# First block's rows fetched ahead and picked on TensorE, and the last expert block's results by token

## What is computed

```python
x = x + mix @ w_out                     # mix = [mLSTM(h) | pool(h)], h = rmsnorm(x, norm1_g) @ w_in
x = x + hier_moe(rmsnorm(x, norm2_g))   # top-1 group, top-2 experts in it
y = rmsnorm(x, norm_f_g)

def hier_moe(x, ...):
    gates = ...                          # (B, L, 16), two entries of a token are not zero
    for e in range(16):
        hid = silu(x @ w_gate[e]) * (x @ w_up[e])      # width 512
        y = y + gates[..., e:e + 1] * (hid @ w_down[e])
```

## Time and profile before

| what | us |
|---|---|
| median of 3 runs | 955.98 |
| the profiled execution | 955.15 |
| its span, first to last instruction | 953.5 |
| TensorE busy | 881.4 (92%) |
| DVE busy | 435.6 (46%) |
| GpSimd busy | 370.2 (39%) |
| ScalarE busy | 145.7 (15%) |
| mean granted TensorE clock | 0.966 of full |

### The profile page before, as it was taken

One profiled execution on the slowest core, in us unless ns is written; L12 is line 12 of the kernel. 1 busy time (PEld: TensorE's weight loads), 2 busy tenths in 40 slices (PEclk: granted clock), 3 DMA queues, 4 the chain that ended last, 5 costly groups with the idle time before them and its releaser, 6 DMA issues. The chain is left out here.

```text
span 953.5 us, 16776 instructions
## 1 busy us (share of the span) xinstructions
PE 881.4 (92%) x6367; PEld 758.9 (80%) x6367; DVE 435.6 (46%) x1168; ACT 145.7 (15%) x447; POOL 370.2 (39%) x569
## 2 busy tenths in 40 slices
PE   5999999999999999999986799999999999999920
PEld 3975969779596795968853399999999999999920
DVE  2245474737537365463656723334333333333255
ACT  2123122221312212121121000000000000000051
POOL 4050040300303012030220466678887777764512
PEclk9999999999999999999989799999999999999975
DMA  9931101020300202011065169999999999999882
GB/s 334 287 128 20 49 14 32 1 78 2 70 8 12 67 1 56 1 13 44 1 192 173 50 212 312 343 348 359 336 350 343 332 334 329 321 310 301 244 326 114
DMA packets 90713, 163.27 MB, mean 171 GB/s; under 512 B 48834, under 2 KB 59570, under 8 KB 82463
## 3 DMA queue, kind: packets, MB, share of 16 engines
q1 hardware_dynamic: 72047, 138.25, 41.4%
q0 software_dynamic: 17568, 24.23, 11.1%
q10 hardware_dynamic: 1040, 0.00, 0.1%
HBM read 139.39 MB, written 25.44 MB: 173 GB/s over the span
## 5 line engine op out<-in xcount | busy, mean ns | idle before, releaser
L1428 PE MATMUL bank<-wout,win 128*128 128x130 f32 (+3 forms) x2048 | 246.4, 282 | 3.2 <-DVE wout L1316 3.2
L1428 PEld LDWEIGHTS bank<-wout,win 128*128 128x128 f32 x2048 | 244.8, 191 | 3.2 <-DVE wout L1316 3.2
L1428 PE MATMUL bank<-hT,win 128*128 128x128 f32 (+1 forms) x1536 | 182.9, 279 | 0.0
L1428 PEld LDWEIGHTS bank<-hT,win 128*128 128x128 f32 x1536 | 178.6, 192 | 1.5 <-issue 1.2
L582 POOL DMA_INDIRECT z_d<-wout,win x75 | 119.2, 1589 | 27.9 <-issue 26.6
L1428 PE MATMUL bank<-win 128*128 128x130 f32 (+3 forms) x1024 | 123.7, 281 | 0.0
L1428 PE MATMUL bank<-win,hT 128*128 128x260 f32 (+3 forms) x512 | 119.9, 412 | 3.2 <-DMA win<-in_w_in 1.7
L1428 PEld LDWEIGHTS bank<-win 128*128 128x128 f32 x1024 | 122.3, 190 | 0.0
L1428 PE MATMUL bank<-wout,mixT 128*128 128x512 f32 (+1 forms) x384 | 116.8, 487 | 1.8 <-ACT mixT L819 1.7
L1428 PEld LDWEIGHTS bank<-win,hT 128*128 128x128 f32 (+1 forms) x512 | 76.1, 171 | 41.8 <-issue 32.7
L1428 PEld LDWEIGHTS bank<-wout,mixT 128*128 128x128 f32 (+1 forms) x384 | 50.8, 163 | 57.1 <-issue 54.4
(11 more groups left out here) (296 smaller groups left out, 813.1 us busy)
## 6 DMA issues: line engine op xcount, KB each, us to landing
win<-in_w_gate SPq DMA_DIRECT2D x32, 1024.0 KB
win<-in_w_up SPq DMA_DIRECT2D x32, 1024.0 KB
win<-in_w_down SPq DMA_DIRECT2D x32, 1024.0 KB
win<-in_w_in SPq DMA_DIRECT2D x4, 2048.0 KB, 19.6
xbuf<-in_x_prompt SPq DMA_DIRECT2D x8, 512.0 KB, 3.9
wout<-in_w_out SPq DMA_DIRECT2D x1, 4096.0 KB, 15.5
z_d<-xbuf SPq DMA_DIRECT2D x32, 128.0 KB
h_d<-xn SPq DMA_DIRECT2D x8, 512.0 KB, 2.8
```

The lines of the kernel that those rows point to most:

```text
L1428: return nc.tensor.matmul(out, lhsT, rhs, start=first, stop=last)
```

## The change

Two things are done, with what they need.

**Block 1's rows.** GpSimd reads the ids of block 1 and gathers its rows after tile 6's scatter, into a buffer of its own (xg1). Rows that belong to tiles 7 and 8 are not in them: their slots still point to the zero row. DVE transposes (first_turn) and scales (first_scale) these during tile 8's mixing. For tiles 7 and 8 a selection matrix is made in places (first_picks on DVE: 1/rms where a token's place is this slot), and TensorE multiplies x1 (copied by ScalarE into xp) with it, which gives the missing columns already transposed; DVE adds both (first_rows), ahead of the table. The rows of h2_d for tiles 7 and 8 are filled with x beforehand by one DMA, and GpSimd's first wait counts that one too. The zero rows are written from one column of the empty table. The state copies go from DVE to ScalarE, and the stores of the states from SyncE's queue to ScalarE's; the state transposes stand in the wait for the routing of tile 8, and WARM is gone.

**The last block.** Its down projection has the tokens on the partitions: hid is the stationary operand, the weights are moved in 512 columns, for two tiles of 120 and 30 rows. DVE adds gate times result to the gathered rows of z_d straight from PSUM; last_d and its transfers are gone. The gathered rows are brought into plain order by eight copies first, and this wait (base_in) now stands ahead of the outputs.

```diff
-    last_d = nc.dram_tensor("last_d", [BLOCK, D], F32).ap()
...
+        PICKED = (LAST - 1, LAST)
...
+        PICKB = ((2, 0, 3), (3, 3, 6), (0, 6, 8))
...
-        FROWS = (P, BLOCK - P)
+
+        FROWS = ((NP - 1) * RP, RP)
+        FBANK = ((5, 6), (7, 1))
...
-        WARM = 14
...
-                sp.dma_start(rows[TOK, :].rearrange("(p n a) -> p n a", p=P, a=2), empty[:, 0:D // (2 * P), :]
-                             ).then_inc(S["ids_zeroed"], 16)
+                sp.dma_start(rows[TOK, :].rearrange("(p n a) -> p n a", p=P, a=1), empty[:, 0:D // P, 1:2],
+                             allow_slow_non_contiguous=True).then_inc(S["ids_zeroed"], 16)
             load_x(3)
+
+            early = [START[t] for t in PICKED]
+            sp.dma_start(h2_d[min(early):max(early) + P, :], x_prompt[0, min(early):max(early) + P, :]).then_inc(S["ids_zeroed"], 16)
...
+                if t == PICKED[0]:
+                    after(sp, "ids_zeroed", 16 * 4)
...
             after(pool, "hist_ready", 1)
-            after(pool, "ids_zeroed", 16 * 3)
+            after(pool, "ids_zeroed", 16 * 4)
...
+                if i == LAST:
+
+                    after(pool, "h2_stored", 16 * (LAST - 1))
+                    after(pool, "u_done", NT)
+                    load_ids(0)
+                    pool.wait_ge(ids_in, 16)
+                    add_quarter(False)
+                    pool.wait_ge(carried, 1)
+                    gather_tokens(first, xg1)
...
+                if t in PICKED:
+                    a.activation(xp[t - PICKED[0]], xbuf[:, t % 4, :].rearrange("p (f k) -> p k f", k=KD), ACT.Copy
+                                 ).then_inc(xp_ready, 1)
...
+            def first_picks(t):
+
+                i, place = t - PICKED[0], rt[:, 80:81]
+                link(v.scalar_tensor_tensor(out=rt[:, 128 + i:129 + i], in0=oh[:, t, 2, 0:1], scalar=-NEAR, in1=place,
+                                            op0=ALU.mult, op1=ALU.add))
+                v.tensor_scalar(pick[i], place_of[:, :, :], rt[:, 128 + i:129 + i], sm[:, 11:12], ALU.is_equal, ALU.mult
+                                ).then_inc(pick_ready, 1)
...
+            def first_rows():
+                dve.wait_ge(base_scaled, 1)
+                after(dve, "out_done", NT)
+                for n, (b, k0, k1) in enumerate(PICKB):
+                    dve.wait_ge(picked, n + 1)
+                    for k in range(k0, k1):
+                        at = B[b][:, (k - k0) * BLOCK:(k - k0 + 1) * BLOCK].rearrange("p (a i) -> p a i", a=NP)
+                        v.scalar_tensor_tensor(out=xgT[:, k, :, 0:RP], in0=at, scalar=g2m[:, k:k + 1], in1=xgS[:, k, :, 0:RP],
+                                               op0=ALU.mult, op1=ALU.add).then_inc(gx_ready, 1)
...
                     h2_evac(LAST - 1)
+                    first_turn()
                     numerators(LAST)
...
                     routing(LAST - 1)
+                    first_scale()
                     residual(LAST)
...
-            gather_turn(1)
             products(1, SLOTS[0][0])
+            gather_turn(1)
...
+            def add_last(i, c, n_done):
+
+                n, cols = FROWS[i], slice(c * (D // 2), (c + 1) * (D // 2))
+                dve.wait_ge(last_done, n_done)
+                return v.scalar_tensor_tensor(out=fy[i][0:n, cols], in0=B[FBANK[i][c]][0:n, :], scalar=fid[0:n, i, 1:2],
+                                              in1=fy[i][0:n, cols], op0=ALU.mult, op1=ALU.add)
...
             products(nblocks, RP)
+            dve.wait_ge(base_in, 16 * 2)
+            for i, n in enumerate(FROWS):
+                for q in range(NQ):
+                    link(v.tensor_copy(fy[i][0:n, :].rearrange("p (m q i) -> p m q i", m=KD, q=NQ)[:, :, q, :],
+                                       fb[i][0:n, q * PIECE:(q + 1) * PIECE].rearrange("p (m i) -> p m i", m=KD)))
             dve.wait_ge(nf_in, 16)
             outputs(0)
-            results(nblocks, RP, sooner + 2)
+            add_last(1, 0, 1)
+            add_last(1, 1, 1).then_inc(mixed, 1)
             outputs(1)
...
+            add_last(0, 0, 2)
+            add_last(0, 1, 3).then_inc(mixed, 1)
             outputs(2)
...
+                if i == NT + 1:
+                    first_picks(LAST - 1)
+                    state_transposes()
                 if 2 <= i:
                     ranks(i - 2)
+                if i == NT + 1:
+                    first_picks(LAST)
...
+            for half in range(2):
+                pe.wait_ge(hid_ready, 4 * nblocks + FH * (half + 1))
+                pe.wait_ge(w_loaded[4 + half], 16 * nblocks)
+                for c in range(2):
+                    last = by_token(1, c, range(half * FH, (half + 1) * FH))
+            last.then_inc(last_done, 1)
+            for c in range(2):
+                by_token(0, c, range(KF)).then_inc(last_done, 1)
```

More of the change, by code:

```diff
@@ L212, in hymba_step @@
         assert off + KD * NP * 32 <= 15 * D
+        PICKED = (LAST - 1, LAST)
+        xp = [win[:, (15 + i) * D:(16 + i) * D].rearrange("p (k f) -> p k f", k=KD) for i in range(2)]
+        xg1 = win[:, 17 * D:17 * D + NP * PIECE].rearrange("p (a d) -> p a d", a=NP)
+        pick = [win[:, 19 * D + i * BLOCK:19 * D + (i + 1) * BLOCK].rearrange("p (a i) -> p a i", a=NP) for i in range(2)]
+        PICKB = ((2, 0, 3), (3, 3, 6), (0, 6, 8))
         yb = [win[:, t * D:(t + 1) * D] for t in range(NT)]
@@ L406, in _ @@
             after(sp, "table_ready", 1)
[L407 to L417, removed]
-            sp.dma_start(pool_sample[0, 0], uout[:, 1, :]).then_inc(S["stores"], 16)
             nblocks = sp.value_load(tabi[0:1, 2 * (NB + 1):2 * (NB + 1) + 1], min_val=NE, max_val=NB)
@@ L661, in _ @@
             last = row_of(nblocks)
-            for i, n in enumerate(FROWS):
-                pool.dma_start(fid[0:n, i, :], ids_d[bass.ds(last + i * P, n), :]).then_inc(fid_in, 16)
+            pieces = ids_d[bass.ds(last, BLOCK), :].rearrange("(i a) n -> a i n", a=NP)
+            for a in range(NP):
+                i, at = (0, a * RP) if a < NP - 1 else (1, 0)
+                pool.dma_start(fid[at:at + RP, i, :], pieces[a]).then_inc(fid_in, 16)
             pool.wait_ge(carried, 7 * sooner + 13)
             add_block(sooner + 2, RP, 7 * sooner + 13)
-            pool.wait_ge(fid_in, 16 * 2)
+            pool.wait_ge(fid_in, 16 * NP)
             f = [0]
@@ L1046, in places @@
                 v.tensor_tensor(cnt[:, :], B[7][:, NE:2 * NE], cnt[:, :], ALU.add).then_inc(S["rank_read"], 1)
+                if t in PICKED:
+                    first_picks(t)
                 for n in range(2):
@@ L1177, in _ @@
             link(v.tensor_scalar(ecap[:, :], iof[:, 0:NE], float(CAP), None, ALU.mult))
+            for a in range(NP):
+                v.tensor_scalar(place_of[:, a, :], iof[:, 0:RP], float(NP), a - NEAR, ALU.mult, ALU.add)
             p0 = 0
@@ L1248, in _ @@
                     norm_x1(i - 1)
-            after(dve, "ulT_done", 1)
-            for n in range(2):
-                last = v.tensor_copy(uout[:, n, :], B[4 + n][0:HIST, :])
-            last.then_inc(S["ul_out"], 1)
-            after(dve, "nT_done", 1)
-            v.tensor_copy(gt[:, :, :], B[6][0:H, 0:2 * P].rearrange("p (a b) -> p a b", a=2)).then_inc(S["nT_out"], 1)
+            first_rows()
             NJ = NB + 1
@@ L1337, in _ @@
                 dve.sem_inc(signal, credit)
-            first_turn()
             def products(j, r):
```

159 lines of the change are left out of this document (96 added, 63 removed).

## The result

The changed kernel took 979.98 us (median of 4 runs, 978.26 to 983.31) beside 955.48 us for the kernel before on the same chip: ratio 1.0266, 95% interval 1.0246 to 1.0285. Forecast were 951.2 us and a range of 944.5 to 958. The profiled execution took 983.31 us with a span of 981.3 us, 27.8 us more than the span before; what follows accounts for these 27.8 us. TensorE is busy for 884.4 us (881.4 before): the time went into waits and into matmuls at half clock, not into work.

The account below looks back on a forecast made before the run. TensorE hardly waits from 100 to 480 us, so the start, the mixer-to-experts step and the end, where DVE matters, decide. Step 7.1 plus end 3.3 minus start 5.6 gains 4.8 us: 951.2 us, range 944.5 to 958.

Parts of the forecast that it names:

- The start: Before GpSimd's first copy: 256-row copy and 4-byte zero pieces delay GpSimd and TensorE, cost 5.6 us, bounds 2 to 9.4.
- rival D: At the start, the HBM-to-HBM copy moves at 165 GB/s: 955.0 us, no change to measure; chance 0.14.
- B: At the start, the copy is hidden by overlap or dlt has more room: 5.6 us more gained, 945.6; chance 0.12.
- Half clock behind the long idle stretch: At the start, TensorE runs at half clock after standing for dlt: 0.8 us added.
- first_turn: In the step, DVE waits for block 1's gathers ahead of numerators(8): 1.7 us late, bounds 0 and 2.8.
- Rival E: In the step, first_turn waits until 6.3 MB of weights are through: 8.3 us more lost, slower than before; chance 0.10.
- The picks: Between tile 8's rank sums and block 1: selection matmuls and DVE adds let block 1 start 13.8 us earlier.
- Block 2: After block 1 starts: table, ids, gathers, transposition and scaling take 31.2 us; the step keeps 7.1 of its 13.8 us.
- Rival C: In the step, block 2's rows come as if unloaded: 13.4 us gained there, 944.9 us; chance 0.16.
- The estimate of 4.2 us for the last gather: At block 2, gathers wait for a packet of weights, not their backlog: about 4.2 us, the step keeping 9.4.
- The end: From the last block to the final stores: by-token results gain 3.3 us, bounds 1 and 5.
- base_in: At the end, DVE waits for the last block's rows before the outputs; their second gather takes 7.9 us, until 912.3.

Follow-up runs that it names:

- moved first_turn: Changed kernel with 32-byte zero pieces and the 256-row copy issued late, first_turn moved in DVE's order from ahead of numerators(LAST) to behind routing(LAST-1): 952.87 us, ratio 0.9973.
- The hold: Changed kernel with 32-byte zero pieces and late 256-row copy, SP asking for block 2's weights only once block 2's rows are in: 954.69 us, ratio 0.9997.
- the run with both things together: Changed kernel, 32-byte zero pieces, late 256-row copy, first_turn behind routing(LAST-1), block 2's weights held until its ids are in: 950.05 us, ratio 0.9954.
- the last kernel: Kernel with block 2's loads split between ids and rows, plus outputs(0) put ahead of DVE's base_in wait at the end: 942.74 us, ratio 0.9853.
- the split: Changed kernel, 32-byte zero pieces, late copy, first_turn moved; block 2's first-half gate and up loaded after its ids, the rest after its rows: 947.61 us, ratio 0.9912.

## Why the prediction was wrong, point by point

**The start, forecast 5.6 us, bounds 2 to 9.4; measured 22.1.** This is the step that failed. "Small packets passed at 13 ns of an engine each, which is 1.5 us": the rate came from a stretch in which the queue carried small loads, and I carried it over to 4-byte writes as if a price for each packet were all that they cost. The count was right (1792 more) and so, for most, was the price, with a median of 9 ns. What had no term is that the queue stood: SP for 9.85 us in its issue, single 4-byte packets for up to 4.5 us, and load_x(3)'s packets behind them for 1.5 us each instead of 0.16. The pieces cost 17.2 us of GpSimd's start (75.84 to 58.63) and 13.5 us of the time in the kernel before. No row of before showed a 4-byte write, and there my rule was to bound from both sides; I put a single rate and no upper bound of its own. The upper bound of 9.4 belonged to the copy. The copy itself cost 3.4 to 3.6 us of start for 2.6 forecast (rival D's price was not met, B's neither). Half clock behind the long idle stretch was forecast at 0.8; the first eight matmuls of 512 columns behind dlt took 5.55 us for 3.60 and the lateness grew by 2.0.

**first_turn, forecast 1.7 us late with bounds 0 and 2.8; measured 4.8.** The mechanism was named and its size missed. numerators(8) started at 524.85, 4.8 us late once the start's 22.05 are taken off. The gathers were issued when forecast (the last at 492.9 on before's scale, 492.6 forecast), but the last took 9.3 us to its use, not 6.5. And a consequence was not in the sum: TensorE's idle time ahead of the last head made its output sums run at half clock, 2.8 us more. The moved first_turn gave both back. Rival E had the place right and the size wrong: 4.8 and 2.8, not 8.3 at one stroke.

**The picks, right.** From rank sums to block 1 5.47 us measured, 5.2 forecast. Block 1 was 8.1 us earlier, not 13.8, by what first_turn had cost ahead of it.

**Block 2, forecast 31.2 us behind block 1; measured 36.2.** Term by term: table 9.5 (9.7), GpSimd's register loads 2.7 (1.4), ids 7.4 (3.2), add and issue 1.1 (1.2), four gathers 5.2 (5.2), the last gather 6.2 (6.5), transposition and scaling 4.1 (4.0). One term carries most of the miss, the ids (4.2 us); the register loads add 1.3. I had the loaded row, 5.9 us, and took a value near the unloaded one, though I had myself put SP's weights at the same moment. Half clock behind the wait cost 2.2 us (1.65). The hold proved the cause: 2.3 us for the ids without the weights. So the step lost 4.2 us where 7.1 were to be gained. Rival C (rows as if unloaded) is refuted as the change stands; SP's wait makes its rows true and puts the weights in their place. The last gather took 6.2, 9.3 and 8.7 us beside 6.3 MB and 3.3 us beside 2.1 MB: here the rows are late for as long as weights are queued beside them. With 2.1 MB the weights were through at about 556, in the midst of the last gather. The gathers are late from the first on: the first packet of rows starts 4.3 us after the first gather's issue in the changed kernel (582.42 to 586.73), 1.8 us where no weights run beside it (554.89 to 556.69).

The Trainium skill (DMA: Bandwidth & Descriptors, Queues, rings and completion order) lets each DMA engine go round its queues packet by packet. The packets agree: from 553 to 558 us of the run with both things together, GpSimd's queue started 185 packets beside 200 of SP's, so the gathers did not stand behind the backlog of the weights. The estimate of 4.2 us for the last gather, which the prediction drew from this, did not come true (6.2 to 9.3). It had neither the late first packet in it nor the gathers ahead in GpSimd's own queue.

**Among the experts, nothing forecast; 2.6 us lost.** Two waits of TensorE for DVE's products, 2.0 us together, stand in this trace. The other traces with the changed step have between none (the moved first_turn) and 1.7 us of them (the last kernel), the kernel before has none, and their cause is open.

**The end, forecast 3.3 (1 to 5); measured 1.05 in the trace and 2.1 alone.** The term that was off most is base_in: 9.7 us from gather to use, 7.9 forecast. The copies were as forecast, 2.54 us for 2.4.

**The sum.** 22.05 (start) + 4.24 (step) + 2.56 (experts) - 1.05 (end) = 27.8 us. The start alone is out of the range by itself; without its error the result would have been near 965 (959.81 and the 5.6 forecast for it) and still outside.

## What to carry to other kernels

Look at the number and the size of the pieces of every DMA that a wait counts, and above all at an `allow_slow_non_contiguous` that a change adds: a few KB in 4-byte pieces all but stopped a queue, and the load behind it, for over 10 us. And count the packets in the page: the access pattern in the text had pairs of 4 bytes, the queue got 32 bytes at a time, and an experiment was planned on the wrong count. When a change moves a small load (ids, rows) to the same moment as a large one, price it by the row in which it stood beside such a load, or hold the large one by what is left of its own slack; the split that gave each just enough was worth 5.3 us (952.87 to 947.61). And put a wait on another queue's data behind all work that doesn't need it: first_turn and base_in cost 6.9 and some 4 us (3.6 by the traces, 4.9 by the medians) for their places in the order alone.

## What was not expected of the hardware

2 x 1024 writes of 4 bytes to HBM held SP for 9.85 to 11.28 us in one issue, and the DMA engines were occupied for some 12 us at 31 to 44 GB/s, mostly with the load that stood behind those writes. Four times 128 writes of 32 bytes cost nothing that can be measured in the time. In that stretch TensorE stood too, in the midst of a row of matmuls that wait for nothing the profile shows:

```profile
PE bank L1428 <- issue: 8.4, 7, 3.2
```

(TensorE's waits of 50 to 100 us in the kernel before with the 4-byte pieces: total, times, longest. The longest, 3.24 us, stands ahead of dlt, which GpSimd hands over late; the other six, 5.2 us together, lie within the matmuls of the input projection. In the changed kernel there are three, the longest 5.18 us, above.) The kernels whose zeros go in 32-byte pieces have none of these. The traces have packets of 16 KB marked as instructions on a queue of their own; one starts at 58.19 in the kernel before, and in the changed kernel none starts between 52 and 73 us. That the engine's own instructions come through the same stopped DMA engines would fit this; it was argued only, and no run tests it.
